# Prompt attention, odd units: the first head's turned tiles are evacuated between the next unit's two row extremes

## The reference, cut to what matters

```python
DIL_PATTERNS = ((128, 1), (512, 4), (2048, 16))
...
    s = jnp.einsum('bnqhd,bnkhd->bnhqk', qs, kb) + bias
    s = jnp.where(valid[None, :, None], s, -jnp.inf)
    m = jnp.max(s, axis=-1)
    p = jnp.exp(s - m[..., None])
    l = jnp.sum(p, axis=-1)
    acc = jnp.einsum('bnhqk,bnkhd->bnqhd', p, vb)
...
    return num / den[..., None]
```

## Time and profile before

| | us |
|---|---|
| median of 3 runs | 1570.49 (1568.12 to 1574.38) |
| the profiled execution | 1566.13 |
| its span, first to last instruction | 1564.3 |
| PE busy | 1484.0 (95%) |
| DVE busy | 808.6 (52%) |
| ACT busy | 555.9 (36%) |
| POOL busy | 310.4 (20%) |
| prompt attention | from about 448 to 599 of the span |

### The profile page before, as it was taken

One profiled execution on the slowest core, in us unless ns is written; L12 is line 12 of the kernel. 1 busy time (PEld: TensorE's weight loads), 2 busy tenths in 40 slices (PEclk: granted clock), 3 DMA queues, 4 the chain that ended last, 5 costly groups with the idle time before them and its releaser, 6 DMA issues.

```text
span 1564.3 us, 23158 instructions
## 1 busy us (share of the span) xinstructions
PE 1484.0 (95%) x8974; PEld 1276.5 (82%) x8974; DVE 808.6 (52%) x1384; ACT 555.9 (36%) x1046; POOL 310.4 (20%) x362
## 2 busy tenths in 40 slices
PE   7999999998988888998999999999999999999986
PEld 6788888887855556766889999999999999888875
DVE  2333201103866664543456966766676666754555
ACT  4401122212134543442343433333333333544452
POOL 3255420002533323000554010000101000000001
PEclk9999999999999999999999999999999999999998
DMA  6346654527575625993466599989798985877865
GB/s 214 105 131 192 184 183 152 183 93 253 172 241 146 199 71 231 417 402 103 127 191 198 177 185 246 202 229 233 205 234 166 246 199 169 291 239 223 271 230 188
DMA packets 138253, 317.76 MB, mean 203 GB/s; under 512 B 23884, under 2 KB 65116, under 8 KB 132997
## 3 DMA queue, kind: packets, MB, share of 16 engines
q1 hardware_dynamic: 129352, 229.26, 44.0%
q0 software_dynamic: 6976, 71.32, 21.0%
q10 hardware_dynamic: 1824, 15.83, 2.4%
HBM read 254.45 MB, written 137.92 MB: 251 GB/s over the span
## 4 chain that ended last, share of the span: by engine, by line
PE 41%; POOL 4%; DVE 3%; issue 3%; DMA 2%; ACT 1%; SPq 1%; POOLq 0%; ACTq 0%; DVEq 0%
PE y_ps L2697 28%; PE y_ps L2781 4%; PE y_ps L2687 3%; PE x_ps L2781 3%; DMA raw_step<-wt_scratch 2%; POOL xm L1712 1%; POOL h_lo L1726 1%; DVE slot_lo L2420 1%; PE y_ps L1845 1%; DVE y L1810 1%; PE m_ps L2708 1%; PE d_ps L2708 1%; DVE y L2520 1%; PE m_ps L2781 0%; PE d_ps L2781 0%
## 5 line engine op out<-in xcount | busy, mean ns | idle before, releaser
L518 PE MATMUL z_ps<-w_hi,h_hi 128*128 128x512 f32 x488 | 190.6, 391 | 4.3 <-POOL h_lo L335 4.3
L518 PE MATMUL z_ps<-w_lo,h_hi 128*128 128x512 f32 x488 | 189.9, 389 | 0.0
L2697 PE MATMUL y_ps<-h_hi,slot_lo 128*128 128x320 f32 (+1 forms) x560 | 179.7, 321 | 0.0
L2697 PE MATMUL y_ps<-h_hi,slot_hi 128*128 128x320 f32 (+1 forms) x560 | 179.7, 321 | 0.0
L2697 PE MATMUL y_ps<-h_lo,slot_hi 128*128 128x320 f32 (+1 forms) x560 | 179.4, 320 | 0.0
L518 PE MATMUL z_ps<-w_hi,h_lo 128*128 128x512 f32 x432 | 168.1, 389 | 0.0
L131 POOL DMA_DIRECT2D ks_sample<-cache_k_win x60 | 34.0, 568 | 626.3 <-PE y_ps L2697 389.4
L2420 DVE TENSOR_TENSOR slot_lo<-raw_step,slot_hi 128x512 fp32r<-128x512 f32 x132 | 85.3, 687 | 83.8 <-ACT slot_hi L2246 83.7
L518 PEld LDWEIGHTS z_ps<-w_hi,h_hi 128*128 128x128 f32 x488 | 91.6, 188 | 24.4 <-POOL h_lo L335 4.9
L2246 ACT CAST slot_hi<-raw_step 128x512 fp32r<-128x512 f32 x132 | 75.3, 618 | 93.5 <-DMA raw_step<-wt_scratch 35.5
L2697 PE MATMUL y_ps<-s_hi,slot_hi 128*128 128x384 f32 x320 | 107.6, 336 | 0.0
(11 more groups left out here) (359 smaller groups left out, 3191.1 us busy)
## 6 DMA issues: line engine op xcount, KB each, us to landing
ks_sample<-cache_k_win POOLq DMA_DIRECT2D x60, 544.0 KB, 8.7
vs_sample<-cache_v_win POOLq DMA_DIRECT2D x60, 544.0 KB, 11.2
raw<-w_gu SPq DMA_DIRECT2D x20, 1024.0 KB, 16.6
raw_step<-f_scratch SPq DMA_DIRECT2D x66, 256.0 KB, 3.8
K<-cache_k_win SPq DMA_DIRECT2D x8, 2048.0 KB
w_raw<-w_in SPq DMA_DIRECT2D x14, 1024.0 KB
z_scratch<-z_out SPq DMA_DIRECT2D x56, 256.0 KB, 2.3
raw_d<-w_down SPq DMA_DIRECT2D x11, 1024.0 KB, 12.7
```

The lines of the kernel that those rows point to most:

```text
L518: mm = pe.matmul(z_ps[t % 3][:, :], x[:, k, t * 128:t * 128 + 128], w[:, par, k, :], start=(k, n) == first, stop=(k, n) == last)
L2697: mm = pe.matmul(bank[:, 0:cols], w, v[:, k, :], start=fresh and (k, m) == (0, 0), stop=(k, m) == (HK - 1, 2), skip_group_check=True)
```

## The change

In DVE's loop of `prompt_attention`, `evacuate` gets a list of heads. In odd units the copies of the first head are issued between the two row extremes of the next unit; the reciprocal and the second head's copies stay behind the second extreme. Even units keep their order. In the last unit, which is odd and has no extremes behind it, the first head's copies stand ahead of the reciprocal. The other engines' lists are unchanged.

```diff
@@ -1123,8 +1123,8 @@
                     dve.tensor_tensor_reduce(S[:, g % 2, r, 0:n], S_ps[r][:, 0:n], bias[:, h, SEQ - n:SEQ], -1.0, 3e38,
                                              ALU.add, ALU.min, accum_out=least[:, g, r:r + 1]).then_inc(E_ready, 1)
 
-                def evacuate(g):
-                    for r in range(2):
+                def evacuate(g, heads):
+                    for r in heads:
                         for i in range(parts(g)):
                             if not on_act(turn_at(g, r, i)):
                                 n, top = turn_at(g, r, i), min(tile(g) + 1 - 4 * i, 4)
@@ -1162,9 +1162,12 @@
                 for g in range(UNITS):
                     if g < LAST:
                         scores(g + 1, 0)
+                    if g % 2:
+                        evacuate(g, (0,))
+                    if g < LAST:
                         scores(g + 1, 1)
                     reciprocal(g)
-                    evacuate(g)
+                    evacuate(g, (1,) if g % 2 else (0, 1))
                     if tile(g) == PT - 2 and pair(g) < NPAIR - 1:
                         prepare(pair(g) + 1)
                     if g >= 2 and g % 2 == 0:
```

## The result

The changed kernel takes 1575.63 us in the median of 22 runs, the kernel before 1570.45 in as many: a ratio of 1.0033, with a 95% interval from 1.002 to 1.0046, or +5.2 us (3.1 to 7.2). It is a slowdown clear of noise, within 0.5%. Forecast were +4.4 us and 1574.9.

The account below looks back on a forecast made before the run. No engine was taken as full: PE runs a chain of hand-overs. Tiles 1, 3, 5 and 7 gave 1.1 + 1.9 - 0.8 + 2.2 = +4.4 us, 1574.9 on the median (+0.28%), range 1569.5 to 1579.6.

Parts of the forecast that it names:

- The value chosen between bounds: Copy directly behind an extreme starts 0 rather than 0.08 us after it; 0.08 would add 0.8 us over ten units.
- the wait is free: In tiles 1, 3 and 5, the turned bank is ready when the moved copy wants it, so the copy needn't wait.
- Tiles 1 and 3: Later second extreme delays PE's score product of unit g+2: +1.1 us in tile 1, +1.9 in tile 3.
- Tile 5: Last turned group starts 1.08 us earlier, but the second extreme then binds: 0.39 gained in pairs 0 and 3, -0.8 together.
- Tile 7: Late reciprocal delays POOL's diagonals and PE's product behind them: 0.0, +0.9, +0.6, +0.6 us by pair, together +2.2.
- Absorbed by nothing: Behind the prompt-attention stage, everything shifts along, so the whole +4.4 us reaches the end.
- Rival A: Freeing the turned bank sooner is all gain, in tile 5 and tile 7: -3.8 us, 1566.7; chance 0.10.
- B: At tile 7 the reciprocal's way over POOL doesn't bind, so it costs nothing: +2.2 us, 1572.7; chance 0.20.
- Rival C: PE's longer stands drop its clock to 1.2 GHz; nine stands grow, 8.6 us more, 1583.5; chance 0.06.
- within 0.5%: Whole kernel's time differs by no more than about 0.5% (7.9 us) from before; chance 0.89.

Follow-up runs that it names:

- The third profile: The changed kernel, unedited, profiled again; stage 155.4 us, clock high in the first units, falls at 44 and 123 us.
- the first profile: The changed kernel, unedited, in its first profile; span 1578.3 us, stage 157.8 us, clock falls at 47 and 153 us.

## Why the prediction was right, point by point

**The forecast** of +4.4 us lies inside the measured interval, and each term has the sign and nearly the size of its row in the table. What the copies cost was read from before's rows a little too high: a 512-wide copy held the extreme up by 0.60 us (0.64 taken), a 256-wide by 0.33 to 0.34 (0.36 taken). The value chosen between bounds, a copy that starts with the reading of the accumulator, was right in every unit of tiles 1, 3 and 5 but one. That one is tile 1 of pair 0, where "the wait is free" failed:

```profile
456.22 1.11 PE L1215 MATMUL T_ps<-ident,S 128*128 128x128 f32 x4
...
456.82 0.08 DVE L1123 DVE_READ_ACCUMULATOR2_ANT least<- 128x1 f32 x1
...
456.94 0.42 DVE L1134 COPY P_T<-T_ps 128x256 f32<-128x256 f32 x1
...
457.28 0.55 DVE L1123 CUSTOM_DVE_ANT_0 S<-S_ps,bias_p 128x384 f32<-128x384 f32 x1
```

The turns ran at the low clock there and the second of the first head's two ended at 456.91, so the copy stood 0.12 for its bank and the extreme came 0.46 later, not 0.34. That pair's +0.45 hides the error, for it made up for the prices that were too high. The third profile, with a high clock there, has no such stand. And the whole of the measured 5.2 us isn't hand-overs: that +4.4 comes close to it is in part luck, since the forecast has the clock at nothing and the hand-overs 0.4 too high, while about one fall of the clock, 1.7 us by the estimate above, came with the change.

**Tiles 1 and 3:** right but for that wait, and shown by the kernel with these tiles alone. The diagonals, which already bound the product with ones in tile 1, moved along and cost nothing of their own: PE stood 0.43 to 0.44 us for them as before.

**Tile 5:** right in mechanism, a gain that the second extreme cuts short; 1.0 instead of 0.8 (0.44 instead of 0.39 in two pairs, 0.10 instead of nothing in one).

**Tile 7:** right, and the least obvious term: the cost isn't where the copies moved but one engine further, over the reciprocal and POOL. In pair 0 the gain of 0.27 at the score product is lost again at the product with ones. The kernel with the reciprocal first shows that this path alone, with what it holds in tile 1, is 3.5 us.

**Absorbed by nothing:** the time from the stage's end to the end of the span is 965.7 to 968.8 us in the kernel before and 965.7 to 970.6 in the changed one. It isn't shorter with the change, so nothing shows that the stage's growth is made up for; a difference of 1 us or so can't be told from four profiles each.

**Rival A** fell at tile 5, **B** at tile 7. **Rival C** didn't come as written, with nine falls and 1583.5, but the argument against it failed. I gave it 0.06 and argued that the grown stands, at most 1.5 us, stay under a stand of 1.7 that the clock had survived. Neither half is good: the longest grown stand was 1.8 us (pair 2, tile 3, from 1.19 before, a row that I hadn't read), and the length of one stand isn't what decides. Nor did nine stands grow: the three of tile 5 (to 0.57, 0.90 and 0.57 us, from nothing) and the one before the product with ones in pair 0 (0.20 to 0.47) are more. In the changed kernel the clock held behind the 1.6 us for ScalarE's copy and behind the 1.78, and fell near 45 us behind 1.31; in the kernel before that stand was 0.98 and it fell in none of four profiles. The price of a fall, put at 0.95 for one score product alone, was 1.5 to 1.7 us (once, at the stage's end with tile 7 alone, 2.9), as the low clock lasts over the following product with ones, the values and the turns. Two falls of 1.6 stay under the bound of 7.9 together with the 4.0 only narrowly, 7.3 in the stage of three profiles; so "within 0.5%" was less sure than my 0.89.

## What to carry to other kernels

Before an instruction is moved ahead on an engine that isn't full, list everything that it passes and who waits for each; here a wait for a bank was shortened by 3.9 us and two others lengthened by 8.7. The instruction to look for is the short one with a long way behind it: behind a reciprocal of 0.16 us lay a way of 1.7 us over POOL to PE, which made half of the change's cost. And an order can be had that gives both: first what a slow engine needs, last what itself waits, and a copy between only where the freed bank is what PE stands for.

## What the runs showed of the hardware that I had not expected

Small changes of PE's stands went with another clock in this stage. With a stand 0.33 us longer in one unit (0.98 to 1.31) the granted clock fell from 2.4 to 1.2 GHz at the same place in each of four profiles, and also in the kernel with tiles 1 and 3 alone; PE had been busy 1.69 us of the 3 from 494 to 497 in the first profile, and the clock fell at 498.7. The one stand isn't the cause by itself. With the reciprocal first the stand there is 1.38 us and the clock held; gone is the stand of 0.44 us for the diagonals, right behind that score product. So the clock fell near 45 us where the two stands add up to 1.75 us and held where they made 1.42 (before) or 1.38. That isn't a rule for other places: in pair 3 the same two stands make 1.86 us and the clock held there in three profiles of the changed kernel and fell in one. What decides stays open.

A fall cost 1.5 to 1.7 us here, and once 2.9. A product with ones that took 0.66 us at the high clock took up to 1.12 where it fell.

The kernel before differs by up to 3.3 us between profiles within this one stage, from the clock alone: whether and for how long it is low in the first units (up to 2.0 us) and whether it falls at 96 to 98 us (1.6 to 1.7). Two single profiles whose stages differ by this much say nothing of an edit; from unit to unit outside these two places, PE's starts agree between them within 0.1 us.
